# One half of a value slab moved one quarter earlier, behind the variance, in a decoder step

## The reference

```python
h = h + 0.5 * swiglu(rms_norm(h))                      # feed-forward 1, width 5632
u = rms_norm(h) @ w_in                                  # q | k | v | conv value, conv gate
# attention: 8 heads, two maps each; prompt causal, samples over 2048 cached keys in 16 pages
w = softmax(s1) - lam * softmax(s2);  o_attn = rms_norm(w @ v) * g_subln * (1 - lam_init)
# convolution, per block c of 128 channels
x = value * sigmoid(gate)
y = depthwise_conv(x, 31 taps) + b
y = silu((y - mean(y)) * rsqrt(var(y) + eps) * g + b)   # mean, variance over the block
h = h + concat(o_attn, o_conv) @ w_out
h = h + 0.5 * swiglu(rms_norm(h))                      # feed-forward 2
h = h + (p @ w_ple_proj) * sigmoid(rms_norm(h) @ w_ple_gate)
```

## Time and profile before

| | before |
|---|---|
| median of 3 runs | 2706.02 us (2701.25 to 2708.99) |
| the profiled execution | 2704.98 us, span 2703.2 us |
| TensorE (PE) busy | 2612.5 us, 97% of the span |
| weight load (PEld) busy | 2545.3 us, 94% |
| VectorE (DVE) busy | 1498.6 us, 55% |
| ScalarE (ACT) busy | 943.3 us, 35% |
| GpSimd (POOL) busy | 351.5 us, 13% |
| transfers | 506.42 MB, mean 187 GB/s over the span |

### The profile page before, as it was taken

One profiled execution on the slowest core, in us unless ns is written; L12 is line 12 of the kernel. 1 busy time (PEld: TensorE's weight loads), 2 busy tenths in 40 slices (PEclk: granted clock), 3 DMA queues, 4 the chain that ended last, 5 costly groups with the idle time before them and its releaser, 6 DMA issues. The chain is left out here.

```text
span 2703.2 us, 49968 instructions
## 1 busy us (share of the span) xinstructions
PE 2612.5 (97%) x20082; PEld 2545.3 (94%) x20082; DVE 1498.6 (55%) x2101; ACT 943.3 (35%) x1085; POOL 351.5 (13%) x614
## 2 busy tenths in 40 slices
PE   7999999999999999988988899999999999999997
PEld 7999999999999999977777799999999999999997
DVE  5555555555555554357786545555555555555655
ACT  5222222222222342345546433222232222322433
POOL 2000000000000120046687110000000000000323
PEclk9999999999999999999998999999999999999999
DMA  5434444344443457899999644444443444444342
GB/s 231 155 141 155 149 146 154 141 155 149 146 154 141 148 186 271 323 364 369 362 388 352 254 151 156 142 155 143 152 155 141 154 143 151 155 141 154 140 145 81
DMA packets 93267, 506.42 MB, mean 187 GB/s; under 512 B 10529, under 2 KB 10530, under 8 KB 53474
## 3 DMA queue, kind: packets, MB, share of 16 engines
q1 hardware_dynamic: 92018, 496.59, 50.2%
q0 software_dynamic: 1136, 8.32, 0.9%
HBM read 495.63 MB, written 9.23 MB: 187 GB/s over the span
## 5 line engine op out<-in xcount | busy, mean ns | idle before, releaser
L1659 PE MATMUL bank<-x_hi,w_hi 128*128 128x320 f32 x3456 | 1073.8, 311 | 23.1 <-DVE w_lo L1079 11.4
L1660 PE MATMUL bank<-x_lo,w_hi 128*128 128x320 f32 x3456 | 1071.0, 310 | 0.0
L1661 PE MATMUL bank<-x_hi,w_lo 128*128 128x320 f32 x3456 | 1070.9, 310 | 0.0
L1070 DVE TENSOR_TENSOR w_lo<-raw,w_hi 128x2048 fp32r<-128x2048 f32 x301 | 689.4, 2290 | 296.5 <-ACT w_hi L657 281.3
L657 ACT CAST w_hi<-raw 128x2048 fp32r<-128x2048 f32 x286 | 544.3, 1903 | 799.3 <-PE bank L1661 797.4
L1659 PEld LDWEIGHTS bank<-x_hi,w_hi 128*128 128x128 f32 x3456 | 651.6, 189 | 26.3 <-issue 15.4
L1660 PEld LDWEIGHTS bank<-x_lo,w_hi 128*128 128x128 f32 x3456 | 651.8, 189 | 0.4
L1661 PEld LDWEIGHTS bank<-x_hi,w_lo 128*128 128x128 f32 x3456 | 651.5, 189 | 0.0
L1659 PE MATMUL bank<-mid_hi,w_hi 128*128 128x320 f32 x1408 | 435.3, 309 | 1.0 <-DVE w_lo L1070 1.0
L1661 PE MATMUL bank<-mid_hi,w_lo 128*128 128x320 f32 x1408 | 435.1, 309 | 0.0
L1660 PE MATMUL bank<-mid_lo,w_hi 128*128 128x320 f32 x1408 | 435.1, 309 | 0.0
(11 more groups left out here) (221 smaller groups left out, 2030.6 us busy)
## 6 DMA issues: line engine op xcount, KB each, us to landing
raw<-slabs_ffn SPq DMA_DIRECT2D x264, 1024.0 KB, 4.7
raw<-k_pool SPq DMA_DIRECT2D x128, 512.0 KB, 6.4
raw<-v_pool SPq DMA_DIRECT2D x128, 512.0 KB, 6.2
raw<-slabs_in SPq DMA_DIRECT2D x64, 512.0 KB, 7.4
raw<-slabs_ple SPq DMA_DIRECT2D x18, 1024.0 KB, 4.8
raw<-slabs_out SPq DMA_DIRECT2D x16, 1024.0 KB, 6.6
raw<-slabs_in SPq DMA_DIRECT2D x8, 1024.0 KB, 4.8
h<-x_t SPq DMA_DIRECT2D x4, 640.0 KB, 8.7
```

Source lines behind the costliest of these rows:

```text
L1070: vt.tensor_tensor(w_lo[n % 2][:, :, :], raw[n % 4][:, :].rearrange("p (k n) -> p k n", n=P), w_hi[n % 2][:, :, :].bitcast(F32), ALU.subtr ...
L1659: mm(out, w_hi[w2][:, t, :], xh, start=start, stop=False)
L1660: mm(out, w_hi[w2][:, t, :], xl, start=False, stop=False)
L1661: return mm(out, w_lo[w2][:, t, :], xh, start=False, stop=stop)
```

## The change

In the value quarter of blocks 1 to 7 the first half of the value slab is no longer multiplied behind the transposes. It is multiplied at the end of the quarter before, the no-slab quarter, as the last thing there, behind `conv_var` and `head_sum`. Block 0's value slab stays where it was, as do the second halves and the gate slabs. Other engines' programs, the ring's order and the number of instructions are the same.

```diff
                 for q in range(GROUPS):
                     c, r = position(it, q)
-                    halves = [2 * k + e for k in slabs_at(it, q) for e in range(2)]
-                    halves = halves or [None, None]
+                    halves = [None, None]
+                    if r < 2 and c < 8:
+                        gate = 2 * (16 + 2 * c + r)
+                        halves = [gate, gate + 1] if r or c == 0 else [None, gate + 1]
                     score(it, q)
...
                         conv_var(c - 1)
                     if r == 2 and c < 8:
                         head_sum(c)
+                    if r == 2 and c < 7:
+                        conv_half(2 * (18 + 2 * c))
             b = NB - 1
```

## The result

The changed kernel takes 2711.86 us (median of 17 runs, 2708.64 to 2716.19) against 2707.39 us for the kernel before (17 runs beside them): 1.0016 of it, 95% interval 1.0010 to 1.0023. So the change costs some 4.4 us. The forecast was 1.2 us less; the measured time lies inside the range given, on the other side of the kernel before.

A forecast was written before the change was run, and what follows sets the result against it. Transfers were taken to bound the stretch. Crossings 1 to 7 summed -0.2 - 0.7 + 0 + 0.2 + 0 - 0.8 + 0.3 = -1.2 us, giving 2705 us against a median of 2706.02; range 2697 to 2716.

The forecast's parts named there:

- The bound: Attention and convolution stretch, 1190 to 1475 us: transfers, busy 0.97 of the time, set the pace; the half fills TensorE's gaps.
- What TensorE gains at the crossings: Crossings 1 to 7, no-slab into value quarter: the half fills key waits; 2.7 us gained at 1 and 6.
- the wait for the logarithm: Crossings 2 to 7: the half waits for ScalarE's logarithm in the same bank, 0.25 us each, bounds 0 and 0.53.
- such falls: TensorE's four clock falls to 0.50 in the stretch: closing gaps could end them, some 3 us each, at most 12.
- All of it meets the next wait, that for the second key page of the gate quarter.: Gate quarter: page wait limits TensorE's gain; 0.2, 0.7 and 0.8 us won at crossings 1, 2, 6; none at 3, 5.
- its delay at 1 to 2.8 us: Value quarter: VectorE's score reading, ahead of the gate slab's low halves and next value issue, comes 1 to 2.8 us later.
- Terms of -0.2 at crossing 1 and 0 at 3 and 5: Net change in time at these passages from no-slab into value quarter: 0.2 us won at 1, nothing at 3 and 5.
- the 0.3 of crossing 7: Last passage into a value quarter: key products had not waited, so TensorE is 0.3 us later.
- The rival that the ring runs dry: Five-buffer transfer ring: late key products delay page issues and empty the queue; 2717, or 2724 in full; chance 0.12.
- had seen room: Page issues behind crossing 3: found at 1284.2 against the 1287.0 needed, so the transfer queue would not run dry.
- "It does nothing": Rival: the half merely changes places with waits that the transfers set; 2706 us, chance 0.25.

The follow-up runs named there:

- fill: The changed kernel with VectorE's taps 11 to 14 put ahead of its reading of the scores in the value quarter: 2707.55 us, 0.9999 of the kernel before.
- All_early: The changed kernel; with q above 0 both gate half casts run together, both low halves and the taps precede VectorE's score reading: 2705.22 us, 0.9987; again 2705.03 us, 0.9994.
- even: The kernel before with the half moved at crossings 2, 4 and 6 only: 2705.55 us, 0.9990 of the kernel before.
- split: The changed kernel with the moved half placed between the two key products of the value quarter: 2711.81 us, 1.0022 of the kernel before.

## Why the prediction was wrong

**The bound: right.** The transfers set the pace. In fill the moved half is in place and VectorE is out of its way: the result is the old time, and TensorE waits for pages for 9.9 and 8.4 us, against 10.0 and 9.8 in the kernel before. None of the waits for keys is at a crossing any more, all seven are in gate quarters. That is what the prediction said of the change as a whole.

**What TensorE gains at the crossings, and the wait for the logarithm: right in kind and size.** The half starts 0.17 to 0.65 us late at crossings 2 to 7, 0.23 at four of them, against the 0.25 put down; only the 0.65 of crossing 4 is above the bound of 0.53. The waits for keys at the crossings are gone, and those in gate quarters went from two to five, as forecast. At crossing 1 the changed kernel's trace shows one thing more. TensorE's clock was at its 1.2 GHz level there (granted 0.50) after waits of 1.76 and 3.00 us, and the half, started at 1198.71 and followed by the key products at 1203.77, took 5.06 us instead of 3.69:

```profile
1195.00:1201.00 6.00, 5.82 (x58) 4.86 (x59) 2.84 (x6) 0.89 (x2) 5.42 (x15) 0.50 1.03 416
...
1195.18 1.94 PE L1832 MATMUL bank<-raw,ET 128*32 128x128 f32 x32 [3.00 <-DMA raw<-v_pool]
...
1198.71 0.83 PE L1744 MATMUL bank<-x_hi,wh_hi 128*128 128x320 f32 x1
...
1203.77 1.93 PE L1786 MATMUL bank<-raw,Qb 128*32 128x256 f32 x32
```

This fall does not explain the loss. All_early, with the half moved at the same place, has it too (0.50 over the same stretch) and is no slower than the kernel before. In even it comes without a moved half at crossing 1:

```profile
1195.00:1201.00 6.00, 5.99 (x70) 3.23 (x74) 4.57 (x10) 0.89 (x2) 5.50 (x13) 0.50 1.00 376
```

By the rule of the Trainium skill ("TensorE: Matmul & The Clock Gate", section "HAM oscillation — how this bites in real kernels") closing the gaps could have ended such falls. Here it did not: the changed kernel has five stretches at 0.50 between 1190 and 1475 us, the kernel before four, and the gaps of the value pages, ahead of the half, stayed.

**The step that failed: "All of it meets the next wait, that for the second key page of the gate quarter."** The prediction looked for what the gate quarter of TensorE needs and found only pages. It also needs two results of VectorE's queue. The text named VectorE among those behind the late key products, put its delay at 1 to 2.8 us, and then followed it only to the next issue of value pages. It never asked what else stands behind that reading in VectorE's queue, and who needs it. Measured, VectorE's idle time ahead of the reading rose from 15.9 to 30.3 us, and it cost 4.4 us on a path that the prediction did not have. The delay itself was also put too low at two places. On average over seven crossings the idle time grew by 2.1 us, but at crossings 3 and 7 it went from none to 3.8 us, above the bound of 2.8. The reason given, that VectorE takes the scores up late there, does not hold: in the kernel before it came to them at 1282.29, 0.2 us behind the transposes. At crossing 4, where the low halves stand ahead of the reading, there was no idle time before or after. Terms of -0.2 at crossing 1 and 0 at 3 and 5 came out as waits of 1.9, 1.3 and 1.7 us, the 0.3 of crossing 7 as 1.4.

**The rival that the ring runs dry** had the right sign and the wrong mechanism. Its trigger does show: behind crossing 3 the value pages are issued at 1294.34, 7.5 us behind the key pages, and the transfers are busy for only 0.52 of 1292.5 to 1295, where the prediction had seen room:

```profile
1286.83 3.05 SPq L435 DMA_DIRECT2D raw<-k_pool  x4
1294.34 3.02 SPq L435 DMA_DIRECT2D raw<-v_pool  x4
...
1292.50:1295.00 2.50, 2.50 (x70) 2.11 (x69) 2.50 (x5) 0.00 (x0) 2.33 (x4) 1.00 0.52 205
```

But even has the same late issues at its crossings and costs nothing: behind crossing 2 its key pages come 9.4 us after the value pages ahead of them (4.9 in the kernel before, 7.4 in the changed one), and the next value pages 7.6 us after the key pages, as in the changed kernel. Split repairs the first key issue at all seven crossings and gains nothing. So at one half's delay the empty places at the even crossings cost nothing that the runs could find; at two halves' delay they are a part, of unknown size, of the 39 us. Why the smaller gap is free (it may stand in for one that came later anyway) was not shown. What the late value issues cost at the odd crossings was not separated. They, too, wait for VectorE's low halves; behind crossing 5 split has the transfers busy for only 0.15 of 1372.5 to 1375, ahead of the value pages issued at 1373.78, and fill brings these issues forward together with VectorE's other work, by 1.4 to 2.0 us against the key pages.

```profile
1372.50:1375.00 2.50, 1.94 (x80) 1.67 (x68) 2.47 (x5) 0.00 (x0) 2.33 (x4) 1.00 0.15 38
```

**"It does nothing"** is what fill measures, 0.9999.

## What to carry to other kernels

When work is moved ahead of a product that another in-order engine waits for, list everything that stands behind that wait in the other engine's queue, not only the result itself, and look for who needs each piece next. If there is independent work in that queue, put it ahead of the wait together with the move: here four taps were enough to turn a loss of 4.4 us into nothing. And in a stage that runs at the pace of its transfers, a gap filled elsewhere may give nothing (fill: 0.9999), while a result of another engine that comes late through the same move still costs.

## What was not expected of the hardware

The loss does not grow in step with the delay. With the key products late by one half (3.7 us) the kernel lost 4.4 us; with two halves (7.4 us) it lost 39 us, 5.6 at each crossing, the transfers' share of the stretch fell from 0.97 to 0.89 and TensorE's granted clock from 0.96 to 0.89. How much of that is the ring of five buffers running empty, how much VectorE's lateness and how much the clock was not separated. And 3.5 us of extra VectorE work in four quarters, in an engine that was busy for 224.87 of 285 us, cost some 9 us of 14: a share of 79% was no sign of room.
